# Prompt and sample attention of a decoder layer: who copies the turned probabilities, where the first sample's keys are turned, and how the sample's PSUM banks are laid out

## What is computed

```python
def mla_attend_prompt(q_lat, q_pe, c_kv, k_pe):
    # blocks of Q_BLOCK = 128 queries
    s = (einsum('bqhc,bkc->bhqk', ql_b, c_kv) + einsum('bqhr,bkr->bhqk', qp_b, k_pe)) * MLA_SCALE
    s = where(kpos[None, :] <= qpos[:, None], s, -inf)
    return einsum('bhqk,bkc->bqhc', softmax(s), c_kv)

def mla_attend_sample(q_lat, q_pe, c_kv, k_pe, past_c, past_kpe):
    s_past = (einsum('bqhc,bkc->bhqk', q_lat, past_c) + einsum('bqhr,bkr->bhqk', q_pe, past_kpe)) * MLA_SCALE
    s_new  = where(causal, (... c_kv ... + ... k_pe ...) * MLA_SCALE, -inf)
    pr = softmax(concatenate([s_past, s_new], axis=-1))
    return einsum(pr[..., :P], past_c) + einsum(pr[..., P:], c_kv)
```

## Time and profile before

| what | value |
|---|---|
| median of 3 runs | 1973.4 us (1971.93 to 1977.59) |
| the profiled execution | 1982.43 us |
| its span | 1980.7 us |
| mean granted TensorE clock | 0.967 of full speed |
| TensorE busy | 1828.9 us (92%) |
| VectorE busy | 690.7 us (35%) |
| ScalarE busy | 480.5 us (24%) |

### The profile page before, as it was taken

The page is one execution under the profiler, slowest core; times in us unless marked ns, Lnnn a source line. Parts: engine busy times, 40 slices in busy tenths (PEclk is TensorE's granted clock), DMA queues, the critical chain, the costliest instruction groups (busy, mean ns, idle before and its releaser), DMA issues.

```text
span 1980.7 us, 35917 instructions
## 1 busy us (share of the span) xinstructions
PE 1828.9 (92%) x15591; PEld 1250.5 (63%) x15591; DVE 690.7 (35%) x1300; ACT 480.5 (24%) x832; POOL 112.4 (6%) x115
## 2 busy tenths in 40 slices
PE   6999997997879999898999999999999999999994
PEld 5999997875556699786545554445554544554441
DVE  4437766445467443554321111111111111111113
ACT  4445653341212322633310111110110000000001
POOL 0000003300101000001000000000000000000000
PEclk7999999898989999899999999999999999999997
DMA  7654540214614583437899999999999999999995
GB/s 222 160 133 128 129 119 4 67 35 129 200 54 176 183 245 105 145 96 282 319 375 420 421 424 428 423 393 402 421 422 427 422 424 400 406 423 426 422 423 195
DMA packets 191392, 545.99 MB, mean 276 GB/s; under 512 B 39227, under 2 KB 146844, under 8 KB 163566
## 3 DMA queue, kind: packets, MB, share of 16 engines
q1 hardware_dynamic: 184080, 518.03, 68.5%
q0 software_dynamic: 6768, 26.09, 4.4%
q10 hardware_dynamic: 438, 0.32, 0.1%
HBM read 524.86 MB, written 28.06 MB: 279 GB/s over the span
## 4 chain that ended last, share of the span: by engine, by line
DMA 28%; PE 20%; DVE 1%; issue 1%; ACT 0%; DVEq 0%
DMA w_expert<-in_w_up_dram 28%; PE p_u L2932 8%; PE p_y L2948 4%; PE p_g L2932 4%; PE p_xg L2900 3%; PE p_xgT L2915 1%; PE p_g L2907 0%; DVE w_expert L3102 0%; DVE w_expert L3093 0%; PE p_xgT L2921 0%; PE p_xgT L3007 0%; PE p_y L2955 0%; PE p_xg L3007 0%; PE p_g L3007 0%; DVE y_slots L3048 0%
## 5 line engine op out<-in xcount | busy, mean ns | idle before, releaser
L2932 PE MATMUL p_u<-w_expert,xgT 128*64 128x256 f32 x2048 | 238.0, 386 | 35.2 <-DMA w_expert<-in_w_up_dram 35.2
L2932 PE MATMUL p_g<-w_expert,xgT 128*64 128x256 f32 x2048 | 232.0, 379 | 2.3 <-DMA w_expert<-in_w_gate_dram 1.4
L2932 PEld LDWEIGHTS p_u<-w_expert,xgT 128*64 128x64 f32 x2048 | 147.7, 139 | 118.1 <-DMA w_expert<-in_w_up_dram 44.7
L2948 PE MATMUL p_y<-w_expert,hidT 128*64 128x512 f32 x960 | 219.2, 599 | 0.5 <-DVE hidT L3044 0.5
L2932 PEld LDWEIGHTS p_g<-w_expert,xgT 128*64 128x64 f32 x2048 | 147.0, 137 | 89.3 <-issue 18.5
L2900 PE MATMUL p_xg<-low,slot_sel 128*64 128x512 f32 x768 | 177.8, 598 | 0.0
L2948 PEld LDWEIGHTS p_y<-w_expert,hidT 128*64 128x64 f32 x960 | 66.7, 137 | 126.7 <-issue 126.0
L3037 DVE CAST row<-rowf 128x1 int32<-128x1 f32 x32 | 4.9, 154 | 356.6 <-POOLq L3174 356.6
L3122 ACT ACTIVATE act_g<-p_g 128x256 f32<-128x256 f32 x32 | 12.3, 384 | 450.7 <-PE p_u L2932 450.7
L2900 PEld LDWEIGHTS p_xg<-low,slot_sel 128*64 128x64 f32 x768 | 52.6, 137 | 80.6 <-issue 74.1
L426 PE MATMUL in_acc<-x_high,w_in_high 128*128 128x320 f32 (+2 forms) x560 | 93.9, 321 | 8.2 <-ACT w_in_high L458 8.2
(11 more groups left out here) (591 smaller groups left out, 2490.6 us busy)
## 6 DMA issues: line engine op xcount, KB each, us to landing
w_expert<-in_w_gate_dram SPq DMA_DIRECT2D x64, 2048.0 KB, 23.0
w_expert<-in_w_up_dram SPq DMA_DIRECT2D x64, 2048.0 KB, 25.1
w_expert<-in_w_down_dram SPq DMA_DIRECT2D x60, 2048.0 KB, 20.4
w_in_raw<-in_w_in_dram SPq DMA_DIRECT2D x32, 1024.0 KB, 5.8
ho_raw<-in_w_out_dram SPq DMA_DIRECT2D x12, 1024.0 KB, 7.0
q_lat<-in_w_out_dram SPq DMA_DIRECT2D x4, 1024.0 KB, 7.9
mem_k_s<-in_cache_mem_k_dram SPq DMA_DIRECT2D x8, 512.0 KB, 7.0
mem_v_s<-in_cache_mem_v_dram SPq DMA_DIRECT2D x8, 512.0 KB, 11.7
```

Of the source, the lines that this page charges most:

```text
L2932: mm = pe.matmul(acc[SL * h:SL * h + SL, 0:FF // 2], xgT[:, t, g // 2, :], w[g][:, FF * t + FF // 2 * h:FF * t + FF // 2 * h + FF // 2], s ...
L2948: mm = pe.matmul(p_y[SL * h:SL * h + SL, 512 * b:512 * b + 512], hidT[:, j, g, :], tile, start=(g == 0 and j == 0), stop=(g == 1 and j == 1))
```

## The change

In the prompt stage, `keep_turned` is gone: ScalarE copies all four heads of a group in two copies, each with its own signal, and TensorE waits for the second only ahead of head 2. VectorE turns the keys of sample 0 there, blocks 0 to 4 ahead of `largest(2)` and 5 to 9 ahead of `largest(3)`. They are put into the third pair of page buffers (`first_keys`), so GpSimd gathers only samples 0 and 1 in the prompt stage, and sample 2 when TensorE has used the last key block of sample 0.

In the sample stage VectorE therefore starts with the keys of sample 1 (six blocks, `largest(0)`, four blocks), then for each b `sums(b-1)`, `largest(b)`, `store(b-2)`, and the keys of b+1. The scores of the new keys move into free columns of the score banks (`p_n`), and the bank that this frees takes the turned rows (`p_r`). `turn_rows(b-2)` moves from between key blocks 5 and 6 to behind the new keys. The small transpose of the new keys' probabilities goes ahead of the eight large ones and is copied first. The last value matmul (256 columns on output partitions 0 to 63) becomes two of 128 columns, on partitions 0 to 63 and 64 to 127. Behind the last sample `turn_rows(6)` and `turn_probabilities(7)` change places. The number that bounds the gather's rows is put into a register once in each stage.

```diff
@@ -1639,7 +1639,7 @@
-        turned = sem("p_turned"); tv = sem("p_turn_v"); ta = sem("p_turn_a"); made = sem("p_made"); ov = sem("p_out_v")
+        turned = sem("p_turned"); ta = sem("p_turn_a"); made = sem("p_made"); ov = sem("p_out_v")
@@ -1662,8 +1662,9 @@
-                for b in range(NBUF):
-                    gather_pages(pool, d, S, b)
...
+                for b in range(NBUF - 1):
+                    gather_pages(pool, d, S, b, last_row)
@@ -1687,17 +1688,16 @@
-                        pe.wait_ge(tv, g)
-                        pe.wait_ge(ta, g)
+                        pe.wait_ge(ta, 2 * g)
...
-                    pe.wait_ge(tv, g + 1)
-                    pe.wait_ge(ta, g + 1)
...
+                        if x % 2 == 0:
+                            pe.wait_ge(ta, 2 * g + x // 2 + 1)
@@ -1729,12 +1729,13 @@
-                def keep_turned(g):
-                    i = GROUPS[g][0]
-                    dve.wait_ge(turned, g + 1)
-                    if g >= 1:
-                        dve.wait_ge(made, g)
-                    dve.tensor_copy(probT[:, 0:2, 0:i + 1, :], p_t[:, 0:512].rearrange("p (x b n) -> p x b n", x=2, b=2)[:, :, 0:i + 1, :]).then_inc(tv, 1)
+                def turn_first_keys(parts):
+                    for c in parts:
+                        if c == 0:
+                            dve.wait_ge(S.lat_in[0], 16)
+                        if c == 8:
+                            dve.wait_ge(S.rope_in[0], 16)
+                        turn_key_block(dve, S, 0, c, first_keys(S, c)).then_inc(S.key_turned, 1)
@@ -1744,10 +1745,12 @@
+                    if g == 1:
+                        turn_first_keys(range(0, 5))
+                    if g == 2:
+                        turn_first_keys(range(5, NCB))
...
-                    keep_turned(g)
-                    if g < 3:
@@ -1767,29 +1770,40 @@
-                    act.copy(probT[:, 2:4, 0:i + 1, :], p_t[:, 512:1024].rearrange("p (x b n) -> p x b n", x=2, b=2)[:, :, 0:i + 1, :]).then_inc(ta, 1)
+                    for u in range(2):
+                        act.copy(probT[:, 2 * u:2 * u + 2, 0:i + 1, :], p_t[:, 512 * u:512 * u + 512].rearrange("p (x b n) -> p x b n", x=2, b=2)[:, :, 0:i + 1, :]).then_inc(ta, 1)
...
+def first_keys(S, c):
+    home, at = (S.lat[NBUF - 1], 512 * c) if c < 8 else (S.rope[NBUF - 1], 512 * (c - 8))
+    return home[:, :, :].rearrange("p k n -> p (k n)")[:, at:at + 512]
+def turn_key_block(dve, S, b, c, dst):
+    src = S.lat[b % NBUF][:, :, 32 * c:32 * c + 32] if c < 8 else S.rope[b % NBUF][:, :, 32 * (c - 8):32 * (c - 8) + 32]
+    return dve.transpose(dst.rearrange("p (k n) -> p k n", n=32), src)
...
@@ -1798,14 +1812,15 @@
...
-        p_s = ps("ps_s", (128, 2048))[:, :].rearrange("p (a n) -> p a n", a=4)[:, :, 0:256]; p_pt = ps("ps_pt", (128, 1024)); p_n = ps("ps_n"); p_o = ps("ps_o")
...
+        score_banks = ps("ps_s", (128, 2048))[:, :].rearrange("p (a n) -> p a n", a=4); p_s, p_n = score_banks[:, :, 0:256], score_banks[0:64, 0, 256:320]
+        p_pt = ps("ps_pt", (128, 1024)); p_r = ps("ps_r"); p_o = ps("ps_o")
...
@@ -1816,9 +1831,13 @@
-                for b in range(NBUF, NB):
-                    pool.wait_ge(made, b - NBUF + 1)
-                    gather_pages(pool, d, S, b)
...
+                for b in range(NBUF - 1, NB):
+                    if b < NBUF:
+                        pool.wait_ge(key_used, NCB)
+                    else:
+                        pool.wait_ge(made, b - NBUF + 1)
+                    gather_pages(pool, d, S, b, last_row)
@@ -1827,59 +1846,61 @@
+                        keys = kT[:, c, :] if b else first_keys(S, c)
...
-                                ins = pe.matmul(p_s[64 * half:64 * half + 64, a, :], S.q_parts[c][quad, 64 * b:64 * b + 64], kT[quad, c, 256 * half:256 * half + 256], start=(c == 0), stop=(c == NCB - 1))
+                                ins = pe.matmul(p_s[64 * half:64 * half + 64, a, :], S.q_parts[c][quad, 64 * b:64 * b + 64], keys[quad, 256 * half:256 * half + 256], start=(c == 0), stop=(c == NCB - 1))
...
-                    if b:
-                        pe.wait_ge(masked, b)
...
-                        pe.matmul(p_n[0:64, 0:64], qs[:, ci, :, :].rearrange("p h t -> p (h t)"), S.c[:, ci, SEQ:T], start=(ci == 0), stop=False)
-                    pe.matmul(p_n[0:64, 0:64], qps[:, :, :].rearrange("p h t -> p (h t)"), S.kp[:, SEQ:T], start=False, stop=True).then_inc(scored, 1)
+                        pe.matmul(p_n, qs[:, ci, :, :].rearrange("p h t -> p (h t)"), S.c[:, ci, SEQ:T], start=(ci == 0), stop=False)
+                    pe.matmul(p_n, qps[:, :, :].rearrange("p h t -> p (h t)"), S.kp[:, SEQ:T], start=False, stop=True).then_inc(scored, 1)
+                def turn_rows(b):
+                    pe.wait_ge(rows, b + 1)
+                    if b:
+                        pe.wait_ge(stored, b)
+                    for ci in range(2):
+                        ins = pe.matmul(p_r[:, 64 * ci:64 * ci + 64], o_rows[:, 128 * ci:128 * ci + 128], S.table("eye2"), start=True, stop=True)
+                    ins.then_inc(o_turned, 1)
...
+                    if b:
+                        pe.wait_ge(rows, b)
+                    pe.transpose(p_o[0:64, 384:448], p_new[:, :], S.ident[0:64, 0:64]).then_inc(p_turned, 1)
...
-                        if j == 3:
+                        if j % 4 == 3:
...
-                    if b:
-                        pe.wait_ge(stored, b)
-                    pe.transpose(p_o[0:64, 384:448], p_new[:, :], S.ident[0:64, 0:64]).then_inc(p_turned, 1)
...
+                    pe.wait_ge(new_copied, b + 1)
...
-                        if j == 0:
-                            pe.wait_ge(new_copied, b + 1)
...
-                            pe.matmul(p_o[64 * half:64 * half + 64, 0:KVL], probT[:, j, 64 * half:64 * half + 64], lat[b % NBUF][:, 8 * half + j, :], start=(j == 0), stop=(j == 7 and half == 1))
-                    pe.matmul(p_o[0:64, 0:KVL], p_newT[:, :], S.c_tok[0:64, 2, :], start=False, stop=True).then_inc(made, 1)
-                def turn_rows(b):
-                    pe.wait_ge(rows, b + 1)
-                    for ci in range(2):
-                        ins = pe.matmul(p_o[:, 256 + 64 * ci:256 + 64 * ci + 64], o_rows[:, 128 * ci:128 * ci + 128], S.table("eye2"), start=True, stop=True)
-                    ins.then_inc(o_turned, 1)
+                            pe.matmul(p_o[64 * half:64 * half + 64, 0:KVL], probT[:, j, 64 * half:64 * half + 64], lat[b % NBUF][:, 8 * half + j, :], start=(j == 0), stop=False)
...
+                        ins = pe.matmul(p_o[64 * half:64 * half + 64, ch], p_newT[:, :], S.c_tok[0:64, 2, ch], start=False, stop=True)
+                    ins.then_inc(made, 1)
...
-                    past(b, range(0, 6))
+                    past(b, range(NCB))
+                    new_keys(b)
...
-                    past(b, range(6, NCB))
-                    new_keys(b)
...
+                turn_probabilities(NB - 1)
...
-                turn_probabilities(NB - 1)
@@ -1898,18 +1919,15 @@
-                        if b:
+                        if b >= 2:
...
-                        src = lat[b % NBUF][:, :, 32 * c:32 * c + 32] if c < 8 else rope[b % NBUF][:, :, 32 * (c - 8):32 * (c - 8) + 32]
-                        dve.transpose(kT[:, c, :].rearrange("p (k n) -> p k n", n=32), src).then_inc(key_turned, 1)
+                        turn_key_block(dve, S, b, c, kT[:, c, :]).then_inc(key_turned, 1)
...
-                    dve.wait_ge(exped, b)
-                    dve.tensor_tensor(new[:, :], p_n[0:64, 0:64], S.table("own_causal")[0:64, 64 * b:64 * b + 64], ALU.add).then_inc(masked, 1)
-                    step(dve.tensor_reduce(stat[:, b % 2, 0:1], p_s, AX.XY, ALU.max))
-                    dve.wait_ge(masked, b + 1)
+                    dve.tensor_reduce(stat[:, b % 2, 0:1], p_s, AX.XY, ALU.max)
+                    step(dve.tensor_tensor(new[:, :], p_n, S.table("own_causal")[0:64, 64 * b:64 * b + 64], ALU.add))
@@ -1926,15 +1944,16 @@
-                    dve.tensor_copy(S.o_lat[:, :, :, SEQ + ND * b:SEQ + ND * b + ND], p_o[:, 256:384].rearrange("p (c h t) -> p c h t", c=2, h=MH)).then_inc(stored, 1)
-                turn_keys(0, range(NCB))
-                for b in range(NB):
+                    dve.tensor_copy(S.o_lat[:, :, :, SEQ + ND * b:SEQ + ND * b + ND], p_r[:, 0:128].rearrange("p (c h t) -> p c h t", c=2, h=MH)).then_inc(stored, 1)
+                turn_keys(1, range(0, 6))
+                largest(0)
+                turn_keys(1, range(6, NCB))
+                for b in range(1, NB):
+                    sums(b - 1)
+                    largest(b)
...
-                    largest(b)
-                    if b:
-                        sums(b - 1)
@@ -1952,16 +1971,16 @@
-                        act.wait_ge(p_turned, 2 * b)
+                        act.wait_ge(p_turned, 3 * b)
...
-                    act.wait_ge(p_turned, 2 * b + 1)
```

(36 more changed lines are left out.)

7 lines of the change are left out of this document (4 added, 3 removed).

## The result

The changed kernel takes 1957.93 us (median of 4 runs, 1955.33 to 1960.08), the kernel before 1973.38 beside it: ratio 0.9914, 95% interval 0.9898 to 0.9930, 15.4 us less. Forecast were 1959.0 and 14.4 less. The profiled execution took 1960.08 us, span 1958.3, mean granted clock 0.974. Against the profiled execution before that is 22.4 us. From the first prompt matmul to the first of `heads_out` it is 165.51 against 149.70 us, 15.8 less. The rest lies elsewhere: behind the attention it is 1297.4 against 1304.9 us, 7.4 less, at a granted clock of 0.99 against 0.98, and in front of it 0.8 more. The medians, 15.4 apart, do not show this rest. "L1853" and the like are now lines of the changed kernel.

The account below looks back on a forecast made before the run. Bounds: in the prompt stage TensorE's waits for VectorE's copies and the low clock behind gaps, in the sample stage TensorE from sample 1. 3.0 + 4.3 + 1.6 - 0.5 + 6.0 = 14.4 us off 1973.4 gave 1959.0 us, range 1952 to 1967.

Parts of the forecast that it names:

- Group 0: Prompt stage, first group: values start after ScalarE's first copy, with hold and low clock partly gone; 3.0 us saved.
- Groups 1 to 3: Rest of the prompt stage: last values end 5.2 us earlier, taken as 4.3 with half a low spell off.
- rival (a): Attention: only the waits go, not the small terms, and the clock stays low behind group 0; 1966.0 us, chance 0.15.
- First sample: Start of the sample stage: sample 0's keys are ready, so its scores end earlier; 1.6 us saved.
- The moved gather: Sample stage: sample 2's gather, now issued there, may add one TensorE stop; -0.5 us.
- Small terms: Samples 1 to 7: rows 2.6, copies 1.6, last value matmul 1.6, tail 0.2; 6.0 us saved.
- the last matmul: End of each sample's values: two matmuls of 128 columns may run side by side; 0.2 us a sample, 1.6 saved.
- The rows: Sample stage: turn_rows outside the key blocks costs 0.50 us instead of 0.93; 0.43 in six samples, 2.6 saved.
- The copies: Sample stage: copying the small transpose first shortens TensorE's wait for p_newT; 0.2 us a sample, 1.6 saved.
- Rival (c): Prompt group 1: VectorE stops for a late gather with largest(2) queued behind it; slower, 1980 us, chance 0.03.
- Rival (b): Behind the attention: the gain is given back in later stages; 1973 us, chance 0.07.
- Rival (d): Attention: a busy TensorE holds the high clock throughout, also on last values and first sample; 1954.1 us, chance 0.13.

Follow-up runs that it names:

- e2: The kernel before with only sample 2's gather moved from the prompt stage to the sample stage: 1973.71 us, ratio 0.9993.
- e3: The changed kernel without early keys, sample 0's keys turned at the start of the sample stage again: 1960.69 us, ratio 0.9923.
- e1: The kernel before with only the copies changed, ScalarE copying all four heads of a prompt group: 1963.97 us, ratio 0.9947.
- e11: The kernel before, unchanged, run once more on a fourth chip: 1962.69 us, ratio 0.9997.
- e7: The changed kernel with key blocks 5 to 7 moved from ahead of largest(3) to between largest(2) and normalize(2): 1949.48 us, ratio 0.9942.
- e9: The changed kernel with both e7's moved key blocks and e8's filling matmuls: 1949.14 us, ratio 0.9933.
- e10: The changed kernel with the turned probabilities copied by VectorE and ScalarE again, all else kept: 1958.55 us, ratio 0.9986 against the kernel before.
- e0: The changed kernel run again on a third chip: 1952.48 us, ratio 0.9958 against the kernel before.
- e8: The changed kernel with eight unused matmuls between the scores of sample 0 and sample 1: 1956.28 us, ratio 0.9913.
- e5: The changed kernel with one last value matmul of 256 columns instead of two of 128, on another chip: 1951.12 us.
- e6: The changed kernel without the gathers of samples 3 to 7, which use the pages of samples 0 to 2, on another chip: 1946.51 us.

## Why the prediction was right

The sum said 14.4 us, the medians 15.4, the attention in the two profiles 15.8. The mechanism was right in the prompt stage and the first sample; that the sum came so close is in part luck, as an error of 3.5 us one way and one of 2.1 the other largely cancel. By its steps:

- **Group 0**, 3.0 (1.5 to 4.5): measured 4.6, from the starts of the transposes of group 1, which moved from 22.83 to 18.25 us behind the stage's first matmul. That is the upper end. The wait for VectorE, the hold and the low clock all went, and not half of them. In these profiles the hold came only with the third gather (gone in e2 and in e3, still there in e1), and it is missing on the chip of e11 even with it. What holds ScalarE up was not found.
- **Groups 1 to 3**, 5.2 without and 4.3 with half a low spell: from those transposes to the end of the last values it was 51.01 - 22.83 = 28.18 us, and is 41.00 - 18.25 = 22.75: 5.4 less. The lateness of `largest(3)` was put at 1.2 us and was 0.8 (0.90 less the usual 0.10); removing it gives back 0.75 (e3, e7). No low spell fell on the last values in the profile after, but one did in e9 (43.44 against 41.80 in e7), 1.6 us. So half a spell was a fair price and this profile the better half.
- **Low spells before.** Against rival (a) the prediction held that the clock fell only behind gaps of 3.7 and 4.1 us in its rows. The same trace has it at the 1.2 GHz level behind the shorter gaps too: behind 2.71 us in group 1 (values 3.58 us long instead of 2.02), 2.54 in group 2 (5.35 instead of 3.81) and 2.35 ahead of sample 0's keys. The prediction counted one spell on the values of groups 1 and 2, and there were two. So five spells of 3.4 us lie in the attention before and one of 6.8 in the attention after. The gap alone does not decide: a spell fell on the last values of e9 behind idle times of 0.95 and 0.77 us, none in the change behind 1.69 and 0.77. Windows of the kernel before:

```profile
538.00:540.00 2.00, 2.00 (x12) 2.00 (x12) 1.40 (x2) 0.24 (x2) 0.00 (x0) 0.56 0.90 299
...
550.00:552.00 2.00, 1.78 (x8) 1.78 (x9) 0.42 (x3) 1.68 (x8) 0.00 (x0) 0.50 0.00 0
...
564.00:566.00 2.00, 2.00 (x48) 1.19 (x41) 2.00 (x5) 0.00 (x0) 0.00 (x0) 0.50 0.00 0
```

- **The split copies against the Trainium skill.** e10 settles what the earlier trace rows said: with VectorE copying half, the prompt stage is 6.5 us longer. The Trainium skill, "TensorEngine Tiling (Array Packing)", section Performance Considerations, recommends both engines for emptying PSUM. Here VectorE's copy stands behind the whole of `largest` in its queue, and starts 2.2 us after ScalarE's (523.49 and 525.69 in e10). No run of this case shows the split with VectorE free. Nearest to it is group 3 of the kernel before, where no `largest` stands in front: TensorE idled 1.04 us ahead of the values there, against 0.77 with both copies on ScalarE.
- **First sample**, 1.6 (0.8 to 2.5): 11.73 to 9.32, 2.4. No low spell fell on its scores.
- **The moved gather**, -0.5 for a further stop: stops went from 18 to 20 (8.1 to 8.5 us), so that much held. But its cause in the text, one stop more per gather in flight, is no general rule, as e0 and e11 have next to none (0.3 and 0.8 us in 2 each). What the step left out: "the softmax stays as it is, also its low spell". The spell became about 6.8 us long instead of 3.4. The first key block of sample 2 came 12.88 us behind that of sample 1, against 12.26 before, in spite of the shorter work. Filling the gap gives back 2.2 us (e8). The length is not the change's doing, though: e5 is the same kernel up to there, and its spell, about 558.7 to 562.1, is 3.4 us long. Windows of e5:

```profile
558.00:560.00 2.00, 2.00 (x63) 1.85 (x54) 1.21 (x5) 0.00 (x0) 0.00 (x0) 0.66 1.03 434
560.00:562.00 2.00, 2.00 (x49) 1.77 (x41) 0.00 (x0) 0.00 (x0) 0.00 (x0) 0.50 0.84 348
562.00:564.00 2.00, 2.00 (x73) 1.61 (x58) 0.00 (x0) 0.00 (x0) 0.00 (x0) 0.98 0.12 45
```

- **Small terms**, 6.0: this is the one that was too large. The five periods from sample 2 to 7 fell from 13.67 to 13.09, 2.9 us in all. The last sample and the tail gave 1.1, and the spell above took 0.6 back: 101.22 - 97.83 = 3.4. Of the parts, the last matmul was right, 0.20. The rows were put at 0.43 and gave 0.19: ten key blocks take 4.50 us, not 4.35, and rows between the new keys and `p_new` cost 0.59, not 0.50. The two matmuls thus still cost 0.59 at the new place; how much of that is the change of form no run shows. The copies were put at 0.2 and gave 0.05: from the first transpose to the values it was 1.65 (661.15 to 662.80), and is 1.59 (647.07 to 648.66). The wait is now for `low` and as long, 0.33 instead of 0.39: the first large copy is as late as the small one was. Rows, copies and last matmul make 0.45 us a sample, which is what e11 and e6 differ by, on chips without the stops (11.74 and 11.29). The first chip shows 0.58, and the 0.13 more were not explained.

The two errors: prompt and first sample gave 12.4 where 8.9 were forecast, samples 1 to 7 3.4 where 5.5 were. Rival (c) did not come: VectorE found the gathered pages in place in the prompt stage. Rival (b) did not either. Rival (a) failed in group 0, held partly in the small terms. Rival (d) was right for the prompt and the first sample, and wrong behind the softmax.

Open is the size on chips without the stops: e0 against its own before gains 8.9 us in medians. Profiles of e0 and e11, taken on two chips, differ by 12.6 in the attention. The step from 15.8 to 12.6 is seen: without the hold the prompt stage before is 50.67 us instead of 52.56, so 1.9 less is to be won, and samples 1 to 7 gain 1.9 instead of 3.4, of which about 1.4 goes to the gathers that come late (e0 against e6). What separates 8.9 from 12.6 was not found.

## What to carry to other kernels

A copy shared by two engines ends with the one that has the longer queue ahead of it: look at when each half starts, not at how long it takes, before giving it to both. When an engine's idle time in front of a wait is used for other work, compare the work with the gap; with three blocks behind `largest(2)` and two ahead of `largest(3)` nothing was lost, where five ahead of `largest(3)` cost 0.75 us. Small terms that rest on a distance between two starts should be priced at the new place too, since part of what a matmul or a copy cost at the old place turns up at the new one: here 0.19 of 0.43 us was won with the rows, and 0.05 of 0.2 with the copy.
